# Second feed-forward layer in seven half-size products, with the first layer's result passed through memory

## What is computed

```
    h = x + merged @ p['w_out']
    hn = rms_norm(h, p['norm_ff_g'])
    ff = jnp.square(jax.nn.relu(hn @ p['w_ff1'])) @ p['w_ff2']
    return h + ff
```

## Time and profile before

| | us |
|---|---|
| median of 3 runs | 2374.62 (2374.56 to 2374.67) |
| profiled execution, from the first to the last instruction | 2372.7 |
| beyond the profiled span, in the median | 1.9 |
| feed-forward, from the first rectified group to the last add | 1490 to 2368 |
| of it, the second layer (eight stretches) | 448 |

### The profile page before, as it was taken

How to read it: one execution, slowest core, us unless ns; L and a number is a source line. 1 busy time by engine, 2 the same in 40 slices (tenths; PEclk the granted TensorE clock), 3 DMA queues, 4 the chain that set the end, 5 groups by cost and what they waited for, 6 DMA issues and landing times.

```text
span 2372.7 us, 33148 instructions
## 1 busy us (share of the span) xinstructions
PE 2313.7 (98%) x12930; PEld 1963.5 (83%) x12930; DVE 1166.5 (49%) x1752; ACT 848.5 (36%) x1480; POOL 39.6 (2%) x64
## 2 busy tenths in 40 slices
PE   8999999899998999999899999999999999999999
PEld 6888888788877888888788888888888888888887
DVE  6333455567636666778676445333333333333333
ACT  6533222366655554667333323302121111212120
POOL 0000000111100000000000000000000000000000
PEclk9999999999999999999999999999999999999999
DMA  4333321656538767888652410111111111111112
GB/s 166 102 124 123 127 90 66 159 140 167 129 113 240 219 224 248 266 257 247 240 186 84 169 46 27 45 36 36 39 41 35 35 44 35 35 36 44 35 35 97
DMA packets 176620, 272.22 MB, mean 115 GB/s; under 512 B 11379, under 2 KB 127987, under 8 KB 173852
## 3 DMA queue, kind: packets, MB, share of 16 engines
q1 hardware_dynamic: 160060, 258.00, 34.2%
q0 software_dynamic: 16480, 13.13, 2.8%
HBM read 200.07 MB, written 73.12 MB: 115 GB/s over the span
## 4 chain that ended last, share of the span: by engine, by line
PE 50%; DVE 1%; ACT 0%; DMA 0%; issue 0%; DVEq 0%
PE acc L146 17%; PE acc L147 17%; PE acc L148 17%; DVE xn_lo L1862 1%; DVE xn_lo L1860 0%; DMA merged<-s_y_T 0%; ACT xn_hi L1853 0%; PE acc L2136 0%; DVE gates L1981 0%; DVE h_T L2087 0%; ACT sums L2188 0%; ACT sums L2191 0%; ACT L2191 0%; ACT gates L2061 0%; DVE gates L2231 0%
## 5 line engine op out<-in xcount | busy, mean ns | idle before, releaser
L146 PE MATMUL acc<-xn_hi,w_hi 128*128 128x512 f32 (+1 forms) x1944 | 693.5, 357 | 25.0 <-DVE xn_lo L615 9.3
L147 PE MATMUL acc<-xn_hi,w_lo 128*128 128x512 f32 (+1 forms) x1944 | 690.9, 355 | 0.0
L148 PE MATMUL acc<-xn_lo,w_hi 128*128 128x512 f32 (+1 forms) x1944 | 689.6, 355 | 0.0
L146 PEld LDWEIGHTS acc<-xn_hi,w_hi 128*128 128x128 f32 x1944 | 368.9, 190 | 80.5 <-issue 16.2
L148 PEld LDWEIGHTS acc<-xn_lo,w_hi 128*128 128x128 f32 x1944 | 368.9, 190 | 51.8
L147 PEld LDWEIGHTS acc<-xn_hi,w_lo 128*128 128x128 f32 x1944 | 369.2, 190 | 51.3
L176 ACT ACTIVATE w_hi<-w_raw 128x1024 fp32r<-128x1024 f32 x146 | 153.6, 1052 | 550.1 <-PE acc L148 509.7
L146 PE MATMUL late_acc<-xn_hi,w_hi 128*128 128x512 f32 (+1 forms) x768 | 286.8, 373 | 3.0 <-DVE late_result_a L865 1.9
L148 PE MATMUL late_acc<-xn_lo,w_hi 128*128 128x512 f32 (+1 forms) x768 | 274.3, 357 | 0.0
L147 PE MATMUL late_acc<-xn_hi,w_lo 128*128 128x512 f32 (+1 forms) x768 | 273.8, 356 | 0.0
L147 PE MATMUL acc<-u_hi,w_lo 128*128 128x512 f32 (+1 forms) x768 | 273.6, 356 | 0.0
(11 more groups left out here) (218 smaller groups left out, 2225.1 us busy)
## 6 DMA issues: line engine op xcount, KB each, us to landing
w_raw<-in_w_tiles SPq DMA_DIRECT2D x146, 512.0 KB, 3.7
c_w<-s_ac SPq DMA_DIRECT2D x20, 1024.0 KB, 4.9
s_late_T<-late_result_s SPq DMA_DIRECT2D x20, 640.0 KB, 6.8
c_grown<-s_grown SPq DMA_DIRECT2D x40, 256.0 KB, 5.7
gates<-s_late_T SPq DMA_DIRECT2D x16, 512.0 KB, 4.1
s_late_T<-late_result_a SPq DMA_DIRECT2D x12, 640.0 KB, 5.9
c_xbc<-s_xbc_T SPq DMA_DIRECT2D x10, 768.0 KB, 5.3
s_xbc_T<-x_T_sb SPq DMA_DIRECT2D x11, 640.0 KB, 3.0
```

What stands on the lines that cost most here:

```text
L146: pe.matmul(out, w_hi, x_hi, start=first, stop=False)
L147: pe.matmul(out, w_lo, x_hi, start=False, stop=False)
L148: return pe.matmul(out, w_hi, x_lo, start=False, stop=last)
```

## The change

The second layer is no longer done block by block. Inner tiles (even and odd), tokens (first and second 640) and output features (first and second 512) are each cut in halves, and the product of the 2 x 2 half-matrices is made with seven products of halves in place of eight (`PRODUCTS`). One entry names the quarters of the weights and how they are combined, which stored operand of features goes with them, and into which quarters of the result the product is added or subtracted. There are 16 pairs of inner tiles, so a product is 16 steps, and a step is one pair: 128 inner features x 512 outputs x 640 tokens, which is 8 units of 320 tokens, one for each of PSUM's banks (`late_acc`, free by then, gives two).

The first layer runs whole ahead of it, 32 tiles. ScalarE squares once, unrounded, into `m.u`; for each pair VectorE makes five mixed operands (`mix`), and SP stores these and the two plain ones to `t_ops` in memory (`store`). In the second layer SP loads for each step one operand of 128 x 640 (`load_t`) and one or two weight quarters of 128 x 512 (`load_w`); VectorE combines two quarters (`add_quarters`), ScalarE rounds both operands, VectorE makes both remainders. At a product's end ScalarE copies the eight banks to SBUF (`copy`), and VectorE adds them into `m.h` in steps 4 to 11 of the next product (`result`). The weights of the second layer come from an input laid out anew (`w_ff2`).

```diff
-    BLOCKS, KB, TILES = FF // 512, 4, 8
-    U1, U2 = NG * 4, NG * KD
+    TILES, PAIRS, HALF, UNIT = FF // P, FF // P // 2, T // 2, T // 4
+    PRODUCTS = (
+        ((0, 3), ALU.add, 0, ((0, 0, ALU.add), (1, 1, ALU.add))),
+        ((1, 3), ALU.subtract, 4, ((0, 0, ALU.add),)),
+        ((3,), None, 2, ((0, 0, ALU.add), (1, 0, ALU.add))),
+        ((2, 3), ALU.add, 5, ((1, 0, ALU.add), (1, 1, ALU.subtract))),
+        ((0, 1), ALU.add, 6, ((0, 0, ALU.subtract), (0, 1, ALU.add))),
+        ((0,), None, 1, ((0, 1, ALU.add), (1, 1, ALU.add))),
+        ((0, 2), ALU.subtract, 3, ((1, 1, ALU.add),)))
...
+        def store(p):
+            sp.wait_ge(self.mixed, p + 1)
+            sp.dma_start(self.t_ops[0:5, p].rearrange("j p t -> p j t"), m.mixed[:]).then_inc(self.mixed_out, 16)
+            for e in range(2):
+                sp.dma_start(self.t_ops[5 + e, p], m.u[:, p % 2, e, H * e:H * (e + 1)]).then_inc(self.plain_out, 16)
+
+        def load_t(n):
+            i, p = n // self.PAIRS, n % self.PAIRS
+            if n < 3:
+                sp.wait_ge(self.mixed_out, 16 * (p + 1))
+            else:
+                sp.wait_ge(self.t_low, n - 2)
+            sp.dma_start(self.t_raw[n % 3], self.t_ops[self.PRODUCTS[i][2], p]).then_inc(self.t_in[n % 3], 16)
+
+        def load_w(n):
...
+            if n < 2:
+                sp.wait_ge(ws.split_done, B_FF + self.TILES - 1 + n)
+            elif n < 4:
+                sp.wait_ge(self.mixed_out, 16 * self.PAIRS)
+            else:
+                sp.wait_ge(self.w_low, n - 3)
...
+        for p in (self.PAIRS - 2, self.PAIRS - 1):
+            store(p)
+        load_w(2)
+        load_w(3)
+        sp.wait_ge(self.plain_out, 32 * self.PAIRS)
+        for n in range(3, self.STEPS):
+            load_t(n)
+            if n > 3:
+                load_w(n)
...
+        for n in range(self.STEPS):
+            i, k = n // self.PAIRS, n % self.PAIRS
+            pe.wait_ge(self.w_low, n + 1)
+            pe.wait_ge(self.t_low, n + 1)
+            for b, bank in enumerate(self.banks):
+                if k == 0 and i:
+                    pe.wait_ge(self.copied, 8 * (i - 1) + b + 1)
...
+                f, cols = b // 2, slice(U * (b % 2), U * (b % 2 + 1))
+                mm = three_products(pe, bank, self.w_hi[n % 4][:, f], self.w_lo[n % 4][:, f],
+                                    self.t_hi[n % 4][:, cols], self.t_lo[n % 4][:, cols], k == 0, k == self.PAIRS - 1)
...
+        act.wait_ge(self.plain_out, 32 * self.PAIRS)
+        for n in range(self.STEPS):
+            i, k = n // self.PAIRS, n % self.PAIRS
+            if n >= 4:
+                if k == 3:
+                    copy(i - 1)
+                self.step_done(act, n - 4)
+            else:
+                act.wait_ge(self.full1, NG * (self.TILES - 1 + n // 2))
+            act.wait_ge(self.t_in[n % 3], 16 * (n // 3 + 1))
+            act.activation(self.t_hi[n % 4], self.t_raw[n % 3], ACT.Identity).then_inc(self.t_high, 1)
...
+            for g in range(NG):
+                rectify(s, t, g, not (isinstance(t, int) and t * NG + g < 2))
+                if g == 0 and mixes and s % 2 == 0:
+                    mix((s // 2 + 1) % 2, pairs_out, t * NG)
...
+        add_quarters(0)
+        for n in range(self.STEPS):
+            i, k = n // self.PAIRS, n % self.PAIRS
+            if n + 1 < self.STEPS:
+                add_quarters(n + 1)
+            j, f = divmod(k - 4, 4)
+            if i and 0 <= j < len(self.PRODUCTS[i - 1][3]):
+                dve.wait_ge(self.copied, 8 * (i - 1) + 2 * f + 2)
+                result(i - 1, j, f, self.staged[:, f], slice(0, H))
+            dve.wait_ge(self.w_high, n + 1)
...
```

More of the change, by code:

```diff
@@ L2110, in __init__ @@
         self.summed, self.logged, self.rooted = (sem("hn_" + n) for n in ("summed", "logged", "rooted"))
-    def sync(self, sp):
[L2113 to L2119, removed]
@@ L2137, in sums_of_squares @@
             mm.then_inc(self.summed, 1)
[L2139 to L2170, removed]
@@ new lines, in scalar, with copy @@
+        for t in range(4):
+            curve(t, t, t > 0, False)
+        with act.Fori(1, self.TILES // 4 - 1) as four:
+            for s in range(4):
+                curve(s, four * 4 + s, True, True, four * 2 + (s // 2 - 1))
+        for t in range(self.TILES - 4, self.TILES):
+            curve(t % 4, t, t < self.TILES - 1, True, t // 2 - 1)
+        def copy(i):
+            for b, bank in enumerate(self.banks):
+                act.wait_ge(self.full2, 8 * i + b + 1)
+                if b == 0 and i:
+                    act.wait_ge(self.added, self.adds_until(i - 1))
+                act.activation(self.staged[:, b // 2, U * (b % 2):U * (b % 2 + 1)], bank, ACT.Identity).then_inc(self.copied, 1)
@@ new lines, in vector, with add_quarters @@
+        for t in range(4):
+            tile(t, t, t > 0, t > 0, None)
+        with dve.Fori(1, self.TILES // 4 - 1) as four:
+            for s in range(4):
+                tile(s, four * 4 + s, True, True, four * 32 + (8 * s - 16))
+        for t in range(self.TILES - 4, self.TILES):
+            tile(t % 4, t, t < self.TILES - 1, True, 16 * (t // 2 - 1))
+        mix(1, 16 * (self.PAIRS - 1), NG * self.TILES)
+        def add_quarters(n):
+            i, k = n // self.PAIRS, n % self.PAIRS
+            quarters, op = self.PRODUCTS[i][0:2]
+            if len(quarters) == 2:
+                dve.wait_ge(self.w_in[n % 4], 16 * (n // 4 + 1))
+                x, y = self.w_raw[n % 4][:, 0:512], self.w_raw[n % 4][:, 512:1024]
+                if quarters == (0, 2):
+                    dve.tensor_tensor(x, y, x, op).then_inc(self.w_sum, 1)
+                else:
+                    dve.tensor_tensor(x, x, y, op).then_inc(self.w_sum, 1)
@@ L2253 @@
+        last = len(self.PRODUCTS) - 1
+        for b, bank in enumerate(self.banks):
+            dve.wait_ge(self.full2, 8 * last + b + 1)
+            result(last, 0, b // 2, bank, slice(U * (b % 2), U * (b % 2 + 1)))
 _SCRATCH = {
```

224 lines of the change are left out of this document (146 added, 78 removed).

## The result

The changed kernel takes 2341.28 us in the median of 4 runs (2337.95 to 2348.27), the kernel before 2374.59 us in the runs beside it (2373.37 to 2374.67): a ratio of 0.9866, 95% interval 0.9853 to 0.9879. It is faster, by 33.3 us where 37.6 were forecast, and inside the range. The profiled execution happens to be the longest of the four (span 2346.5 us, time 2348.27), so its trace is some 7 us longer than the median run.

What follows compares the result with a forecast made beforehand. The prediction took TensorE's instruction stream as the bound. Span 2372.7 - 55.6 (products) + 15.5 (seam) + 2 (clock) = 2334.6 us; with the median 1.9 above the span, 2336.5, rounded to 2337 us; range 2327 to 2362.

Steps and rivals of the forecast that it cites:

- Products: Second layer's matmuls: 2688 of 320 columns at 146 ns, 392.4 us in place of 448.0, a gain of 55.6 us.
- (c): Rival, second layer: leaner matmuls, 133.3 or 135.8 ns for 320 columns, run ending at 2303 or 2310 us; chance 0.04.
- (d): Rival: 320-column matmuls cost 160 ns, no change; or saving fails so or first layer loses cover, 2360 to 2395; chance 0.07.
- First layer: Same matmuls, 13.8 us a tile, with VectorE's mixes and the stores hidden beside them: cost 0.
- Seam: TensorE's pause between the layers: last mix, stores landing, then rounding and remainders of the first operand; +15.5 us, bounds 12.8 and 18.
- half clock: After the pause between the layers TensorE's clock is granted at 0.50 for a while: +2 us, bounds 1.8 and 3.
- Supply of a step: Second layer's loads, roundings, sums and remainders: loop over two steps takes 6.6 us against TensorE's 7.0, 7.3 with an add; cost 0.
- L: Time from a second-layer step's first load issue to its second load's landing, taken as 4.4 us.
- rival (a): Second layer's supply loop binds a little, L 5.1 to 5.8: 2345 us at 5.1, 2365 at 5.6; chance 0.13.
- rival (b): Same supply loop with L over 5.9, loss eating the gain; 2393 us at L of 6.3; chance 0.09.
- Copies at a product's end: ScalarE's copies of eight banks, about 0.42 us each, run while TensorE does the later banks: cost 0.
- End: End of the kernel: last add of 320 columns in place of 256, last store 320 KB in place of 640: cost 0.

Runs made afterwards that it cites:

- the last experiment: Kernel before, second-layer matmuls reading the first layer's operand: 2367.9 us; kernel before, its own operand neither rectified nor squared: 2373.9 us.
- the version with the sum behind: Changed kernel with VectorE's sum of the next step's weight quarters moved behind this step's two remainders: 2335.0 us, ratio 0.9839.
- Covering the seam: Changed kernel, two weight buffers moved, steps 0 and 1 prepared early, loads ahead of last stores: 2332.2 us; with the sum behind the remainders too, 2320.5 us.

## Why the prediction was nearly right

It forecast 2337 us and 2341.3 came out. By its own steps:

**Products.** 146 ns were taken, 146.7 measured, in every product: 394.2 us against 392.4, +1.8. Choosing 32 cycles from the first layer's rows would have given the exact number. The 48 and 24 cycles belonged to an operand that the change does away with (the last experiment), so they were no bound for it. Rivals (c) and (d) are out by the 146.7 ns. The Trainium skill (TensorE: Matmul & The Clock Gate, Back-to-back issue gap) has a formula, for an isolated matmul by its own words, that gives 135.8 ns for 320 columns as an estimate; the stream of matmuls in this trace doesn't agree with it.

**First layer.** Forecast 0: four tiles take 55.12 us as before, with the mixes and stores beside them.

**Seam.** Forecast 15.5, measured 14.7. The timeline of the seam, in the profiled execution of the changed kernel, has its three parts:

```profile
1921.88 0.42 DVE L2344 SCALAR_TENSOR_TENSOR gates<-acc,sums 128x256 f32<-128x256 f32 x1 [2.18 <-PE acc L148]
...
1922.79 3.77 DVE L2336 TENSOR_TENSOR u_mixed<-u_pairs 128x640 f32<-128x640 f32 x5 [0.48 <-ACT u_pairs L2284]
...
1926.58 0.37 SPq L2154 DMA_DIRECT2D s_t_ops<-u_mixed  x1
...
1933.70 0.74 ACT L2311 ACTIVATE t_hi<-gates 128x640 fp32r<-128x640 f32 x1 [10.94 <-DMA s_t_ops<-u_pairs]
...
1936.56 0.61 PE L146 MATMUL acc<-t_hi,w_hi 128*128 128x320 f32 x1 [14.72 <-DVE t_lo L2393]
```

From the last matmul (1921.84) to the store's issue 4.7 us (4.8 forecast), to ScalarE's start 7.1 (7.6), to TensorE's start 2.9 (3.1). The half clock behind it was forecast at 2: the first step takes 5.46 us and not 3.52, 1.9 over. Covering the seam was worth 14.6 us, a little less than the two together. The stores weren't the only limit, as the prediction had it: without ScalarE's wait for them the weights of step 2, which wait for the last mixes' store, hold TensorE nearly as long.

**Supply of a step.** Forecast 0, and this is the term that was wrong: 6.3 us by the median of the version with the sum behind, some 9 in the profiled execution. The condition was right (a loop over two steps, of a landing, 2.0 us of VectorE and 0.15 of hops, and 0.75 more with an add), and the experiments bear it out: taking the sum out of it removes the pauses, lengthening it by 0.60 us adds 22.6 us where the formula gave about 24. The number put into it was wrong. L was taken from a pair of loads of 256 and 512 KB, 4.2 us, plus 0.15 for the larger load. The stretch shows about 5.3, as the weights land in 4.8 to 5.0 us instead of 3.8; by the prediction's own sign, landings over 5 us, the term failed. The argument was that at 58% of the full rate a pair finds the queue empty. The rows show the DMA engines busy for 0.65 of the time at 207 GB/s, and in the stretch at 412 GB/s of the earlier trace rows for all of it. So half the full rate takes two thirds of the engines' time here. The packets differ: 2.6 KB of data each on average in the stretch (17.31 MB in 6577), 5.0 KB in that of the earlier trace rows (4.53 MB in 907).

```profile
DMA packets 7380, 17.31 MB, mean 207 GB/s; under 512 B 803, under 2 KB 803, under 8 KB 7374
```

```profile
DMA packets 1026, 4.53 MB, mean 412 GB/s; under 512 B 119, under 2 KB 119, under 8 KB 1025
```

Nor was the queue empty for most loads. Of the 75 weight loads of 512 KB issued from 1940 us on in the trace of the changed kernel, 13 were issued with no earlier transfer under way but their own step's features, and landed in 4.4 us in the median; the other 62 took 5.0. Meeting other transfers therefore goes with about 0.5 us of the delay. The other 0.6 us is there without it, and its cause is open: these weights come from another input, in two pieces of 2 KB for each partition and not one of 4, beside 320 KB of features and not 256, and no run separates these.

So the mechanism of rival (a) is what happened, with an L inside its range, though the time lies below its 2345 and inside the forecast's own bounds: with L at 5.3 its formula gives 48 x 0.20 + 32 x 0.58 - 14 = 14 us, twice what the medians show. The formula takes every landing at the median; in the trace the buffers' lead takes up much of what is over, and a few late landings, 6 to 8 us, stand behind about half of the 9 us. L is 0.9 us above the 4.4 of the forecast and short of the 5.9 where rival (b) begins. The Trainium skill (DMA: Bandwidth & Descriptors, Latency and other measured facts) has 0.2 us for HBM access on average and 2 us at high load, by estimate 1.8 us more; the 0.9 of these rows is half of that.

**Copies at a product's end.** Forecast 0, measured 3.3 us in the profiled execution (a part of the 9): 2.4 by the loop, as the copies are queued behind a rounding that waits for VectorE's sum, and 0.9 by a rounding whose load came behind a store of the result, a meeting that the forecast did not list. They cost nothing in the version with the sum behind.

**End.** Forecast 0. From the last matmul to the span's end are 4.45 us (2342.05 to 2346.5), and 4.97 before.

**Sum.** The version with the sum behind has a span of 2334.7 us, where the forecast's sum, with supply at 0, was 2334.6; the products' +1.8, the seam's -0.8 and the end's -0.5 nearly cancel. An agreement to 0.1 us is luck, as that version's own runs lie 3.5 us apart. So is part of the nearness of 2337 to 2341.3: the loop's formula, with the L that was measured, would have put the time near 2351.

## What to carry to other kernels

Where one engine both prepares the next step from fresh loads and finishes the current one, look at its order before its busy share: work that waits for a load, queued ahead of work that TensorE needs now, makes a loop of landing and work, and swapping the two lines was worth 6 us here. When such a loop comes out as near its limit as 6.6 of 7.0 us, take the landing from rows that carry the traffic of the new stretch, in pieces of its size, not from a pair of loads on an idle queue. Try two such edits alone and together: by the medians, covering the seam was worth 9.1 us alone and 14.6 with the loop relieved.

## What the runs showed of the hardware

A float32r matmul's start distance depends on which tile holds the moving operand: in the same place of the program, with the same shapes, 512 and 256 columns took 56.00 us per stretch from one tile and 55.20 from another, and a change of the first tile's values left its 56.00. And three matmuls of 512 and three of 128 columns in turn took 1.03 us, where six of 320 take 0.88: 61 us lost by splitting the same columns as 512 + 128 instead of 320 + 320.
